# Gates one block further ahead, exponentials between weight copies, two heads' choice moved up, and GpSimd in place of VectorE for the lower activation parts

## The chip, the cores and the metric

One core of a Trainium2 chip runs the kernel. The metric is device time in microseconds (us), median of three runs, lower is better. TensorE (PE) multiplies, VectorE (DVE) and ScalarE (ACT) work elementwise, GpSimd (POOL) works elementwise and issues indirect DMAs, and SyncE's queue (SP) issues the other DMAs. Each engine runs its own instructions in order and waits on semaphores.

## The reference, cut to what matters

A decoder block on 256 tokens of width 1024: two attention mixers, then the PEER channel mixer, which is most of the time. All in float32.

```python
def chunk_fn(xc):                       # 128 tokens at a time
    q = (xc @ wq).reshape(128, 8, 2, 128)
    sc = einsum('thpd,pkd->thpk', q, subkeys)
    sv, si = top_k(sc, 16)              # 16 of 128 keys, both sides
    cand = sv[:, :, 0, :, None] + sv[:, :, 1, None, :]
    cv, ci = top_k(cand.reshape(128, 8, 256), 16)
    e = i1 * 128 + i2                   # the experts chosen
    g = softmax(cv)
    act = gelu(einsum('td,thkd->thk', xc, u[e]))
    return einsum('thk,thkd->td', g * act, v[e])
```

There are 16384 experts. The kernel gathers none: it multiplies all of `u` by the tokens, takes gelu of all of it, multiplies by a gate (the softmax weight where the expert was chosen, else zero), and multiplies all of `v` by the result.

## The kernel before

**Stages.** The two mixers come first, to about 216 us. Then eight query tiles. Then the 128 tiles of `u` (each 128 experts, 512 KB), to about 659 us, then the 128 tiles of `v`, to about 1066 us. `big` holds the activations of all experts, one block of 256 columns (tokens) for each tile.

**Splits.** Each float32 operand is used as two parts in fp32r. For a weight tile ScalarE copies `raw` to `hi` (`loop_hi`, L1197), VectorE subtracts to get `lo` (`loop_lo`, L1682); three slots (`SPLIT = 3`) rotate, so the copy of tile n waits until TensorE has used tile n-3. For an activation block of the `v` stage ScalarE makes `auxh` (`w_hi_gated`, L1224) and VectorE `auxl` (`w_lo`, L1908), in three slots as well. TensorE does three products: high by high, high by low, low by high (`u_tile` L830 to L832, 24 matmuls; `v_tile` L886, 12 matmuls of 512 columns).

**Router.** From the query tiles to `u` tile 62, VectorE chooses keys and pairs (`choose_keys`, `choose_pairs`, `numbers`, `weights`, `addresses`) in an order written out by hand, with the `lo` copies that are due put between by `spread(n)`. GpSimd adds pairs (L2018) and picks (L2028). ScalarE takes three exponentials (`weights_exp`, L1251), after `u` steps 8, 20 and 51 (`EXP_AT`); each has an activation table load before and after it, since gelu needs another table.

**Gates.** For tokens 128 to 255 GpSimd scatters weights into `gate_d` in memory with 128 indirect DMAs (L2038); in the `v` stage SP loads one 64 KB block a tile into a ring of `GRING = 4` (L355), and `gate_block` (L1922) multiplies the activations by it. For tokens 0 to 127 the gates come from one-hot products: for every four tokens `g_group` (TensorE, L843) multiplies `oneB` (ScalarE: `squares_b` L1212, `relu_b` L1218) by `oneA` (VectorE: `keys_equal` L1844, `rows_a` L1852); VectorE sums (`add_parts` L1860) and multiplies (`weigh` L1867). Groups run through the second half of `u` and the first half of `v`: there one group stands before every second `v` tile (the group stage), and the last 67 tiles have none (the plain stage).

**Order in the `v` stage.** In step j VectorE does `w_lo` of block j+2 (which waits for ScalarE's high part), its share of a group, `loop_lo` of tile j+3, and `gate_block` of block j+3. ScalarE does (in even steps `squares_b`), the high part of block j+2, which waits for that block's gate, (in odd steps `relu_b`), and `loop_hi` of tile j+3. SP issues the load of tile j+4 once the `lo` of tile j is made, then the gate load of block j+4 once block j is gated.

Of the kernel before, what the change touches and what calls it, by code (L numbers as in the profile page):

```python
# [23 lines left out]
F32 = mybir.dt.float32  # L24
F32R = mybir.dt.float32r
U32 = mybir.dt.uint32
ALU = mybir.AluOpType
# [3 lines left out]
P = 128  # L31
D = 1024
T = 256
# [3 lines left out]
NH = 8  # L37
# [32 lines left out]
EXP_AT = (8, 20, 51)  # L70
# [20 lines left out]
def build(nc, x_d, wpre_d, u_d, v_d, par_d, cst_d, kep_d, out_d):  # L91
    with ExitStack() as ctx:
# [157 lines left out]
        def S(name):  # L250
            if name not in N:
                N[name] = sem(name)
            return N[name]
# [664 lines left out]
        def _(act):  # L918
# [333 lines left out]
            def weights_exp(z, b, c0, c1):  # L1252

                act.preload_act_table_set(LN_EXP)
                act.wait_ge(S("router_d"), z + 1)
                of_heads = gwt[:, c0 * 16:c1 * 16]
                act.activation(of_heads, of_heads, ACT.Exp, scale=rs2[:, b:b + 1]).then_inc(S("router_exp"), 1)
                act.preload_act_table_set(GELU)

            def u_steps(j0, j1):  # L1260

                for j in range(j0, j1):
                    u_step(0, j)
# [3 lines left out]
            u_steps(EXP_AT[0], EXP_AT[1])  # L1267
            weights_exp(1, 1, NH + 2, 2 * NH)
            u_steps(EXP_AT[1], EXP_AT[2])
            weights_exp(2, 0, 0, NH)  # L1270
            u_steps(EXP_AT[2], ROUTER - 2)
# [47 lines left out]
        def _(dve):  # L1319
# [483 lines left out]
            choose_keys(0)  # L1803
            sc_out(NH - 1)
            spread(2)
# [3 lines left out]
            spread(3)  # L1809
            choose_pairs(NH, 6)  # L1810
            from_best(NH, NH + 2)
            numbers(NH, NH + 2, 6, 9)
            weights(0, NH, NH + 2)
            dve.wait_ge(S("cleared"), 16 * 16)
            addresses(NH, NH + 2)
# [88 lines left out]
            def w_lo(i, b):  # L1904

                s = (V0 + b) % SPLIT
                dve.wait_ge(S("whi_done"), i * UNROLL + (b + 1))
                dve.tensor_tensor(auxl[:, s * T:(s + 1) * T], big[:, bass.ds(i * (UNROLL * T) + b * T, T)],  # L1908
                                  auxh[:, s * T:(s + 1) * T].bitcast(F32), ALU.subtract).then_inc(S("wlo_done"), 1)

            def w_lo_tokens(b, tb, ready, count, done):

                dve.wait_ge(S(ready), count)
                c0 = (V0 + b) % SPLIT * T + tb * P
                dve.tensor_tensor(auxl[:, c0:c0 + P], big[:, b * T + tb * P:b * T + (tb + 1) * P],  # L1915
                                  auxh[:, c0:c0 + P].bitcast(F32), ALU.subtract).then_inc(S(done), 1)

# [6 lines left out]
            w_lo_tokens(0, 0, "whi_tokens", 1, "wlo_tokens")  # L1924
# [4 lines left out]
            w_lo_tokens(0, 1, "whi_done", 1, "wlo_done")  # L1929
            gate_block(0, 2)  # L1930
            w_lo(0, 1)
# [5 lines left out]
            def v_step(i, j):  # L1937
                w_lo(i, j + SPLIT - 1)
                loop_lo(i, V0 + j + SPLIT)
                gate_block(i, j + SPLIT)  # L1940

            def v_step_g(i, j, keys=True, rows=True):
                g = NGRP + 1 + j // 2
                w_lo(i, j + SPLIT - 1)
                if j % 2 == 0:
                    add_parts(i, g, GT)
                    if keys:
                        keys_equal(i, g + 3, GT)
                else:
                    weigh(i, g, GT)  # L1950
                    if rows:
                        rows_a(i, g + 2, GT)
                loop_lo(i, V0 + j + SPLIT)
                gate_block(i, j + SPLIT)
# [4 lines left out]
            each_tile(dve, HALF - 1, lambda i, j: v_step(i, HALF - 2 + j))  # L1959
            w_lo(0, NBLK - 1)  # L1960
# [8 lines left out]
        def _(pool):  # L1969
# [77 lines left out]
            pool.wait_ge(S("keys_chosen"), 2)  # L2047
            pool.wait_ge(S("router"), 1)
            pool.wait_ge(S("chosen"), 1)
            scatter(3)  # L2050
# [24 lines left out]
            scatter(16 * NH - sent[0])  # L2075

# [120 lines left out]
```

## Time and profile before

| | us |
|---|---|
| three runs | 1070.92, 1072.34, 1072.85 |
| median | 1072.34 |
| the profiled execution, as timed | 1071.63 |
| its span in the trace | 1069.6 |

| engine | busy us | share | instructions |
|---|---|---|---|
| TensorE, matmuls | 1047.1 | 98% | 6814 |
| VectorE | 812.1 | 76% | 1631 |
| ScalarE | 629.8 | 59% | 1128 |
| GpSimd | 332.5 | 31% | 227 |

A matmul's busy time runs to the modelled end of its result, so a TensorE that waits a few tenths of a microsecond between tiles still counts as busy. What a tile costs is read from start to start. The times of the trace count from the start of the span.

### The profile page before, as it was taken

To read this page: it belongs to the slowest core of one execution; us is meant where nothing else is said; L and a number is where in the kernel's file an instruction comes from. 1 tells how busy PE (TensorE), PEld (TensorE's weight loads), DVE (VectorE), ACT (ScalarE), POOL (GpSimd) and SP (SyncE) were. 2 spreads that over 40 slices of the span, in tenths; PEclk is the share of its full clock that TensorE was granted. 3 is DMA by queue.
4 is the path that set the end of the run, shared out by engine and by line. 5 is a ranking of instruction groups with operands and counts; after the bars stand their busy time and mean duration, and the time that the engine had idled before them with its cause. 6 is when DMAs were issued, how large, how long until landed. Compare 5 with 4: busy or idle time off the path is not lost.

```text
span 1069.6 us, 21135 instructions
## 1 busy us (share of the span) xinstructions
PE 1047.1 (98%) x6814; PEld 913.8 (85%) x6814; DVE 812.1 (76%) x1631; ACT 629.8 (59%) x1128; POOL 332.5 (31%) x227
## 2 busy tenths in 40 slices
PE   9999999999999999999999999999999999999998
PEld 7798899999999999999999999766676777777775
DVE  7768886788989988977667667887778876666665
ACT  5557776665455445477667666666666654444443
POOL 0011211036268777876877874000000000000000
PEclk9999999999999999999999999999999999999999
DMA  8674646665456666576766766555555576666553
GB/s 339 245 236 134 203 142 212 197 205 170 157 161 174 173 182 188 166 187 168 176 165 169 177 159 173 178 176 169 168 172 177 177 228 200 202 201 201 199 200 106
DMA packets 89473, 198.20 MB, mean 185 GB/s; under 512 B 26320, under 2 KB 42832, under 8 KB 89424
## 3 DMA queue, kind: packets, MB, share of 16 engines
q1 hardware_dynamic: 68544, 188.99, 53.6%
q0 software_dynamic: 20736, 8.46, 6.9%
q8 instruction: 25, 0.41, 0.2%
q10 hardware_dynamic: 144, 0.14, 0.1%
q14 instruction: 24, 0.20, 0.1%
HBM read 187.01 MB, written 10.55 MB: 185 GB/s over the span
## 4 chain that ended last, share of the span: by engine, by line
PE 57%; DVE 15%; issue 14%; ACT 11%; DVEq 1%; ACTq 1%; DMA 0%
PE bank L830 10%; PE bank L832 10%; PE bank L831 10%; ACT hi L1197 7%; DVE lo L1682 6%; DVE big L1922 3%; ACT auxh L1224 3%; PE bank L384 2%; PE bank L385 2%; PE bank L386 2%; PE bank L450 2%; PE bank L770 2%; DVE gsum L1860 2%; DVE oneA L1852 2%; PE bank L454 1%
## 5 line engine op out<-in xcount | busy, mean ns | idle before, releaser
L1682 DVE TENSOR_TENSOR lo<-raw,hi 128x1024 fp32r<-128x1024 f32 x253 | 320.6, 1271 | 100.4 <-ACT hi L1197 99.7
L1197 ACT ACTIVATE hi<-raw 128x1024 fp32r<-128x1024 f32 x253 | 266.2, 1052 | 155.4 <-PE bank L832 152.4
L830 PE MATMUL bank<-xhi,hi 128*128 128x256 f32 x1024 | 292.4, 286 | 3.5 <-DVE lo L1682 2.3
L832 PE MATMUL bank<-xhi,lo 128*128 128x256 f32 x1024 | 290.6, 284 | 0.0
L831 PE MATMUL bank<-xlo,hi 128*128 128x256 f32 x1024 | 290.4, 284 | 0.0
L2038 POOL DMA_INDIRECT gate_d<-chosen_w,chosen_at x128 | 236.2, 1845 | 73.7 <-issue 48.2
L830 PEld LDWEIGHTS bank<-xhi,hi 128*128 128x128 f32 x1024 | 197.4, 193 | 4.0 <-ACT hi L1197 3.5
L831 PEld LDWEIGHTS bank<-xlo,hi 128*128 128x128 f32 x1024 | 197.2, 193 | 0.0
L832 PEld LDWEIGHTS bank<-xhi,lo 128*128 128x128 f32 x1024 | 197.0, 192 | 0.0
L886 PE MATMUL bank<-hi,auxh 128*128 128x512 f32 x504 | 168.3, 415 | 1.8 <-DVE auxl L1915 0.4
L886 PE MATMUL bank<-lo,auxh 128*128 128x512 f32 x504 | 156.9, 392 | 0.0
L1224 ACT ACTIVATE auxh<-big 128x256 fp32r (+1 forms) x127 | 53.0, 418 | 175.5 <-DVE big L1922 175.5
L886 PE MATMUL bank<-hi,auxl 128*128 128x512 f32 x504 | 155.7, 390 | 0.0
L886 PEld LDWEIGHTS bank<-hi,auxh 128*128 128x128 f32 x504 | 85.1, 188 | 46.3 <-DVE auxl L1908 33.1
L1908 DVE TENSOR_TENSOR auxl<-big,auxh 128x256 fp32r<-128x256 f32 x127 | 54.0, 425 | 83.8 <-ACT auxh L1224 83.8
L886 PEld LDWEIGHTS bank<-lo,auxh 128*128 128x128 f32 x504 | 94.6, 188 | 21.6
L886 PEld LDWEIGHTS bank<-hi,auxl 128*128 128x128 f32 x504 | 94.6, 188 | 21.5
L1330 DVE TENSOR_TENSOR lo<-raw,hi 128x1024 fp32r<-128x1024 f32 x73 | 90.1, 1244 | 26.6 <-ACT hi L931 26.3
L931 ACT ACTIVATE hi<-raw 128x1024 fp32r<-128x1024 f32 x73 | 77.1, 1058 | 46.8 <-PE bank L454 19.2
L1212 ACT ACTIVATE oneB<-kep,eT 128x128 fp32r<-128x128 f32 x256 | 81.1, 389 | 0.0
L384 PE MATMUL bank<-xhi,hi 128*128 128x256 f32 x192 | 56.2, 293 | 0.0
L385 PE MATMUL bank<-xlo,hi 128*128 128x256 f32 x192 | 54.2, 283 | 0.0
(393 smaller groups left out, 1493.2 us busy)
## 6 DMA issues: line engine op xcount, KB each, us to landing
raw<-u_d SPq DMA_DIRECT2D x128, 512.0 KB, 3.4
raw<-v_d SPq DMA_DIRECT2D x128, 512.0 KB, 3.4
raw<-wpre_d SPq DMA_DIRECT2D x70, 512.0 KB, 4.4
gate_d<-big POOLq DMA_DIRECT2D x16, 512.0 KB, 5.4
gring<-gate_d SPq DMA_DIRECT2D x128, 64.0 KB, 3.0
big<-wpre_d SPq DMA_DIRECT2D x8, 512.0 KB, 8.3
gate_d<-chosen_w,chosen_at POOLq DMA_INDIRECT x128
big<-x_d SPq DMA_DIRECT2D x4, 256.0 KB, 4.3
```

The costliest lines, as they stand in the source:

```text
L384: pe.matmul(out, wh, xh, start=(k == 0), stop=False)
L830: pe.matmul(out, wh, xhi[:, k, :], start=(k == 0), stop=False)
L831: pe.matmul(out, wh, xlo[:, k, :], start=False, stop=False)
L832: m = pe.matmul(out, wl, xhi[:, k, :], start=False, stop=(k == KT - 1))
L886: m = pe.matmul(bank[2 * b + f][:, :], a_, w_[:, s, f * 512:(f + 1) * 512], start=(first and st_ == 0), stop=False, skip_group_check=True)
L931: act.activation(hi[:, slot(n), :], raw[:, splits(n) % RING, :], ACT.Copy).then_inc(hi_done, 1)
L1197: act.activation(hi[:, slot(n), :], raw[:, splits(n) % RING, :], ACT.Copy).then_inc(hi_done, 1)
L1212: m = act.activation(oneB[:, g % 2, t, :], iota, ACT.Square, bias=i2, scale=-1.0)
L1224: act.activation(auxh[:, s * T:(s + 1) * T], big[:, bass.ds(i * (UNROLL * T) + b * T, T)], ACT.Copy).then_inc(S("whi_done"), 1)
L1330: dve.tensor_tensor(lo[:, slot(n), :], raw[:, splits(n) % RING, :], hi[:, slot(n), :].bitcast(F32), ALU.subtract).then_inc(lo_done, 1)
L1682: dve.tensor_tensor(lo[:, slot(n), :], raw[:, splits(n) % RING, :], hi[:, slot(n), :].bitcast(F32), ALU.subtract).then_inc(lo_done, 1)
L2038: pool.indirect_dma_start(gate_d, bass.IndirectOffsetOnAxis(chosen_at[:, d:d + 1], 0), chosen_w[:, P + d:P + d + 1], None, compute_op=ALU. ...
```

## The change

Four edits, all of order or place; no operation of the computation is added or taken away.

1. `gate_block` in the `v` stage runs four blocks ahead in place of three; the first four blocks are gated before the loop.
2. `w_lo` and `w_lo_tokens` move from VectorE to GpSimd, after its last scatter.
3. `weights_exp` puts the weight copy of step j between gelu and the table load, and the copy of step j+1 between the exponential and the table load back; the places are 4, 18 and 50.
4. VectorE's pair choice, numbers, weights and addresses of the first two heads come before `choose_keys(15)` and `choose_keys(0)`, with six `lo` copies before their end in place of nine. GpSimd issues five scatters in place of three before it waits for the last keys.

```diff
@@ -67,7 +67,7 @@
 HALF = NBLK // 2
 GRING = 4
 EARLY = 7
-EXP_AT = (8, 20, 51)
+EXP_AT = (4, 18, 50)
 
 
 PARAMS = dict(g2=8, qg=64, kgc=64, kgs=128, posk=16, posv=16, w2k=128, w2v=128, subk=256, gw=192)
@@ -1251,11 +1251,15 @@
             act.wait_ge(S("h_saved"), 16 * TB)
             def weights_exp(z, b, c0, c1):
 
+                j = EXP_AT[z]
                 act.preload_act_table_set(LN_EXP)
+                loop_hi(0, N_PRE + j + SPLIT)
                 act.wait_ge(S("router_d"), z + 1)
                 of_heads = gwt[:, c0 * 16:c1 * 16]
                 act.activation(of_heads, of_heads, ACT.Exp, scale=rs2[:, b:b + 1]).then_inc(S("router_exp"), 1)
+                loop_hi(0, N_PRE + j + 1 + SPLIT)
                 act.preload_act_table_set(GELU)
+                gelu_pair(0, j + 1, 0)
 
             def u_steps(j0, j1):
 
@@ -1264,11 +1268,11 @@
 
             u_steps(0, EXP_AT[0])
             weights_exp(0, 1, NH, NH + 2)
-            u_steps(EXP_AT[0], EXP_AT[1])
+            u_steps(EXP_AT[0] + 2, EXP_AT[1])
             weights_exp(1, 1, NH + 2, 2 * NH)
-            u_steps(EXP_AT[1], EXP_AT[2])
+            u_steps(EXP_AT[1] + 2, EXP_AT[2])
             weights_exp(2, 0, 0, NH)
-            u_steps(EXP_AT[2], ROUTER - 2)
+            u_steps(EXP_AT[2] + 2, ROUTER - 2)
             for j in range(ROUTER - 2, ROUTER):
                 loop_hi(0, N_PRE + j + SPLIT)
             act.wait_ge(S("bank67_read"), 2)
@@ -1800,19 +1804,19 @@
 
             keys_ready()
             spread(1)
-            choose_keys(0)
             sc_out(NH - 1)
-            spread(2)
+            choose_pairs(NH, 4)
+            from_best(NH, NH + 2)
+            numbers(NH, NH + 2, 4, 6)
+            weights(0, NH, NH + 2)
+            dve.wait_ge(S("cleared"), 16 * 16)
+            addresses(NH, NH + 2)
             dve.wait_ge(S("sc_out"), NH)
             choose_keys(2 * NH - 1)
             keys_ready()
-            spread(3)
-            choose_pairs(NH, 6)
-            from_best(NH, NH + 2)
-            numbers(NH, NH + 2, 6, 9)
-            weights(0, NH, NH + 2)
-            dve.wait_ge(S("cleared"), 16 * 16)
-            addresses(NH, NH + 2)
+            spread(8)
+            choose_keys(0)
+            spread(9)
             for z in range(3):
                 choose_pairs(NH + 2 + 2 * z, 12 + 3 * z)
             from_best(NH + 2, 2 * NH)
@@ -1901,47 +1905,29 @@
 
             V0 = N_PRE + NBLK
 
-            def w_lo(i, b):
-
-                s = (V0 + b) % SPLIT
-                dve.wait_ge(S("whi_done"), i * UNROLL + (b + 1))
-                dve.tensor_tensor(auxl[:, s * T:(s + 1) * T], big[:, bass.ds(i * (UNROLL * T) + b * T, T)],
-                                  auxh[:, s * T:(s + 1) * T].bitcast(F32), ALU.subtract).then_inc(S("wlo_done"), 1)
-
-            def w_lo_tokens(b, tb, ready, count, done):
-
-                dve.wait_ge(S(ready), count)
-                c0 = (V0 + b) % SPLIT * T + tb * P
-                dve.tensor_tensor(auxl[:, c0:c0 + P], big[:, b * T + tb * P:b * T + (tb + 1) * P],
-                                  auxh[:, c0:c0 + P].bitcast(F32), ALU.subtract).then_inc(S(done), 1)
-
             def gate_block(i, m):
 
                 dve.wait_ge(gate_in[m % GRING], i * (16 * (UNROLL // GRING)) + 16 * (m // GRING + 1))
                 of_block = big[:, bass.ds(i * (UNROLL * T) + (m * T + P), P)]
                 dve.tensor_tensor(of_block, of_block, gring[:, m % GRING, :], ALU.mult).then_inc(S("gated"), 1)
 
-            w_lo_tokens(0, 0, "whi_tokens", 1, "wlo_tokens")
             add_parts(0, NGRP, GT)
             keys_equal(0, NGRP + 3, GT)
             gate_block(0, 0)
             gate_block(0, 1)
-            w_lo_tokens(0, 1, "whi_done", 1, "wlo_done")
             gate_block(0, 2)
-            w_lo(0, 1)
+            gate_block(0, 3)
             dve.wait_ge(S("bank45_read"), NH + NBLK // 2)
             weigh(0, NGRP, GT)
             rows_a(0, NGRP + 2, GT)
             loop_lo(0, N_PRE + NBLK - 1 + SPLIT)
 
             def v_step(i, j):
-                w_lo(i, j + SPLIT - 1)
                 loop_lo(i, V0 + j + SPLIT)
-                gate_block(i, j + SPLIT)
+                gate_block(i, j + GRING)
 
             def v_step_g(i, j, keys=True, rows=True):
                 g = NGRP + 1 + j // 2
-                w_lo(i, j + SPLIT - 1)
                 if j % 2 == 0:
                     add_parts(i, g, GT)
                     if keys:
@@ -1951,13 +1937,13 @@
                     if rows:
                         rows_a(i, g + 2, GT)
                 loop_lo(i, V0 + j + SPLIT)
-                gate_block(i, j + SPLIT)
+                gate_block(i, j + GRING)
 
             each_tile(dve, HALF - 16, v_step_g)
             for j in range(HALF - 16, HALF - 2):
                 v_step_g(0, j, keys=j < HALF - 8, rows=j < HALF - 6)
-            each_tile(dve, HALF - 1, lambda i, j: v_step(i, HALF - 2 + j))
-            w_lo(0, NBLK - 1)
+            each_tile(dve, HALF - 2, lambda i, j: v_step(i, HALF - 2 + j))
+            loop_lo(0, V0 + NBLK - 1)
             dve.wait_ge(S("h_back"), 16 * TB)
             for z, (b, c, w) in enumerate(out_parts_v):
                 dve.wait_ge(S("sum_ready"), z + 1)
@@ -2044,10 +2030,10 @@
                 pair_sum(c)
             pick(NH)
             pick(NH + 1)
-            pool.wait_ge(S("keys_chosen"), 2)
             pool.wait_ge(S("router"), 1)
             pool.wait_ge(S("chosen"), 1)
-            scatter(3)
+            scatter(5)
+            pool.wait_ge(S("keys_chosen"), 2)
             pair_sum(2 * NH - 2)
             pair_sum(2 * NH - 1)
             scatter(8)
@@ -2074,6 +2060,26 @@
                     scatter(1)
             scatter(16 * NH - sent[0])
 
+            V0 = N_PRE + NBLK
+
+            def w_lo(i, b):
+
+                s = (V0 + b) % SPLIT
+                pool.wait_ge(S("whi_done"), i * UNROLL + (b + 1))
+                pool.tensor_tensor(auxl[:, s * T:(s + 1) * T], big[:, bass.ds(i * (UNROLL * T) + b * T, T)],
+                                  auxh[:, s * T:(s + 1) * T].bitcast(F32), ALU.subtract).then_inc(S("wlo_done"), 1)
+
+            def w_lo_tokens(b, tb, ready, count, done):
+
+                pool.wait_ge(S(ready), count)
+                c0 = (V0 + b) % SPLIT * T + tb * P
+                pool.tensor_tensor(auxl[:, c0:c0 + P], big[:, b * T + tb * P:b * T + (tb + 1) * P],
+                                  auxh[:, c0:c0 + P].bitcast(F32), ALU.subtract).then_inc(S(done), 1)
+
+            w_lo_tokens(0, 0, "whi_tokens", 1, "wlo_tokens")
+            w_lo_tokens(0, 1, "whi_done", 1, "wlo_done")
+            each_tile(pool, NBLK - 1, lambda i, j: w_lo(i, j + 1))
+
     return nc
```

## Rows read from the trace of the kernel before

**Rows 1.** Windows: stretch, its length, busy us (count) per engine, clock, DMA, GB/s
```profile
560.00:655.00 95.00, 95.00 (x799) 95.00 (x798) 66.06 (x92) 66.17 (x123) 73.95 (x42) 1.00 0.70 170
665.00:756.00 91.00, 86.24 (x378) 64.88 (x377) 73.07 (x134) 58.15 (x118) 0.00 (x0) 1.00 0.55 175
869.00:960.00 91.00, 90.96 (x371) 67.02 (x370) 58.21 (x95) 42.13 (x62) 0.00 (x0) 1.00 0.63 203
306.70:310.10 3.40, 3.35 (x16) 3.38 (x17) 3.40 (x8) 0.00 (x0) 3.10 (x2) 0.51 0.68 190
```

**Rows 2.** Timeline, group stage: start, us, engine, line, what [idle <-who]
```profile
695.08 0.42 ACT L1224 ACTIVATE auxh<-big 128x256 fp32r x1 [2.02 <-DVE big L1922]
...
695.40 0.61 ACT L1218 ACTIVATE oneB<-oneB 128x512 fp32r<-128x512 f32 x1
...
696.12 0.64 PE L843 MATMUL bank<-oneA,oneB 128*128 128x128 f32 x4 [0.36 <-issue]
```

**Rows 3.** TensorE's timeline: an unstalled group and tile, and the last group
```profile
663.32 0.56 PE L843 MATMUL bank<-oneA,oneB 128*128 128x128 f32 x4
...
666.53 0.62 PE L886 MATMUL bank<-hi,auxh 128*128 128x512 f32 x2
...
866.38 0.63 PE L843 MATMUL bank<-oneA,oneB 128*128 128x128 f32 x4
...
866.86 0.67 PE L886 MATMUL bank<-hi,auxh 128*128 128x512 f32 x2
```

**Rows 4.** Timeline, plain stage: one tile
```profile
941.15 0.62 PE L886 MATMUL bank<-lo,auxh 128*128 128x512 f32 x2
...
942.49 0.42 ACT L1224 ACTIVATE auxh<-big 128x256 fp32r x1 [1.58 <-DVE big L1922]
...
942.98 0.61 PE L886 MATMUL bank<-hi,auxl 128*128 128x512 f32 x2
...
943.05 0.42 DVE L1908 TENSOR_TENSOR auxl<-big,auxh 128x256 fp32r<-128x256 f32 x1 [0.68 <-ACT auxh L1224]
...
943.53 0.30 PEld L886 LDWEIGHTS bank<-hi,auxh 128*128 128x128 f32 x2 [0.36 <-DVE auxl L1908]
```

**Rows 5.** TensorE's timeline: the last two tiles
```profile
1058.50 0.47 PE L901 MATMUL bank<-hi,auxh 128*128 128x512 f32 x1
...
1061.37 0.47 PE L901 MATMUL bank<-hi,auxh 128*128 128x512 f32 x1 [1.93 <-DVE auxl L1908]
```

**Rows 6.** Groups by line, VectorE, 665 to 756 us: the lower parts
```profile
L1908 DVE TENSOR_TENSOR auxl<-big,auxh 128x256 fp32r<-128x256 f32 x27 | 11.5, 425 | 18.3 <-ACT auxh L1224 18.3
```

**Rows 7.** Timeline: GpSimd's 128x256 subtraction, and a VectorE copy beside GpSimd
```profile
234.90 1.47 POOL L1997 TENSOR_TENSOR xlo<-big,xhi 128x256 fp32r<-128x256 f32 x1 [1.16 <-ACT xhi L949]
...
241.38 0.74 POOL L1997 TENSOR_TENSOR xlo<-big,xhi 128x256 fp32r<-128x256 f32 x1 [0.55 <-ACT xhi L949]
...
292.20 1.76 DVE L1682 TENSOR_TENSOR lo<-raw,hi 128x1024 fp32r<-128x1024 f32 x1
```

**Rows 8.** Timeline, router stage: copy, table load, VectorE's waits, TensorE's stalls
```profile
293.45 1.06 ACT L1197 ACTIVATE hi<-raw 128x1024 fp32r<-128x1024 f32 x1 [1.82 <-PE bank L832]
...
295.01 1.28 ACT L1254 ACT_TABLE_LOAD   x1
...
299.04 1.22 DVE L1682 TENSOR_TENSOR lo<-raw,hi 128x1024 fp32r<-128x1024 f32 x1 [2.18 <-ACT hi L1197]
...
306.75 0.55 PE L830 MATMUL bank<-xhi,hi 128*128 128x256 f32 x1 [1.89 <-DVE lo L1682]
...
337.27 1.98 DVE L1682 TENSOR_TENSOR lo<-raw,hi 128x1024 fp32r<-128x1024 f32 x1 [1.10 <-ACT hi L1197]
...
358.69 0.35 PE L830 MATMUL bank<-xhi,hi 128*128 128x256 f32 x1 [1.25 <-ACT hi L1197]
```

**Rows 9.** Timeline: GpSimd's longest instruction of the router stage
```profile
305.49 3.70 POOL L2038 DMA_INDIRECT gate_d<-chosen_w,chosen_at  x1 [0.30 <-issue]
```

**Rows 10.** DMA issues: what, queue, count, KB each, us to landing
```profile
gring<-gate_d SPq DMA_DIRECT2D x128, 64.0 KB, 3.0
```

## The prediction

> **What bounds the kernel now.** I read the windows first, for each engine's busy share and the clock, then the timeline of one repeated pattern in each stage, then the starts of TensorE's instructions, because its busy time hides waits below half a microsecond.
>
> In the windows [rows 1] the columns after the length are TensorE's matmuls, its weight loads, VectorE, ScalarE and GpSimd. In the second half of `u` (560 to 655 us) TensorE is busy all the time at full clock: nothing there can be gained. In the group stage of `v` (665 to 756) it is busy 86.24 of 91 us, VectorE 73.07, ScalarE 58.15, GpSimd 0. No engine is full, so a chain of waits sets the pace.
>
> The chain is in the timeline [rows 2]. ScalarE has waited 2.02 us for VectorE's gate (L1922), makes the high part (695.08), only then `relu_b` (695.40 to 696.01), and TensorE's group, which needs `relu_b`, starts at 696.12. The page can't name what released it ("issue"), but the order in the code and 0.11 us between them do. So the gate, the last thing that VectorE does in a step, is the first that ScalarE needs in the next.
>
> How much TensorE loses: at the start of the stage, where the operands are ready, a group and its tile last from 663.32 to 666.53, 3.21 us [rows 3]. Within a tile four pairs of matmuls take 942.98 - 941.15 = 1.83 us, so the six pairs of a tile take 2.745 us [rows 4]. A group and two tiles would need 3.21 + 2.745 = 5.955 us. They get (866.38 - 663.32) / 30 = 6.77 us [rows 3].
>
> In the plain stage the same chain is closed without groups [rows 4]: high part at 942.49 after a wait of 1.58 for the gate, lower part on VectorE at 943.05, and TensorE's next tile at 943.53 when the lower part is there. From tile 61 (866.86, [rows 3]) to the last two (1058.50, [rows 5]) are 65 tiles, 191.64 us, 2.948 each against 2.745. TensorE's busy time there reads 90.96 of 91 [rows 1]; only the starts show the 7%.
>
> In the router stage TensorE has two larger stalls, 1.89 us at 306.75 and 1.25 at 358.69 [rows 8]. Behind the first, the clock is 0.51, the lower of the two levels, for 3.40 us [rows 1].
>
> **Gates four ahead, and lower parts on GpSimd.** They act together. Gating a block a step earlier takes gate and high part out of the chain: ScalarE finds the block gated a whole tile (2.7 us) ago, more than the 2.02 that it waited. The gate's data must be there too: its load is issued when the `lo` of tile j is made and is now needed after the `lo` of tile j+3, three tiles (8.2 us) later, against 3.0 us to landing [rows 10]. The line of SP's queue is not changed; what stands behind the gate load there is the next tile's load, and the wait in front of it (block j gated) is met a tile earlier. The gate's work on VectorE is the same.
>
> VectorE gives up 11.5 us of lower parts in 91 [rows 6]. Per group pair (6.77 us) it was busy 73.07 / 91 x 6.77 = 5.44; without 0.86 it is 4.58. GpSimd has nothing else in this stage. Its 128x256 subtraction of the same shapes took 0.74 us alone and 1.47 when a copy on VectorE ran [rows 7], and a VectorE copy beside GpSimd took 1.76 against 1.22 alone [rows 7, 8]: the two wait for one another, about 0.54 us on VectorE's side for one operation of GpSimd. Bounds for a pair: two lower parts cost VectorE from 0 (they fall into its waits) to 2 x 0.74 = 1.48. I take two collisions, 1.08, since the rows with a copy running are the nearest: 4.58 + 1.08 = 5.66, below 5.955. The rest of ScalarE fits (58.15 / 91 x 6.77 = 4.33). In the plain stage VectorE has 58.21 / 91 x 2.95 = 1.89 a tile, less 0.43, plus 0.54, so 2.00 below 2.745.
>
> Latency, not only throughput: a slot's new high part follows the weight copy that waits for TensorE to leave tile n-3, so it has two tiles, 5.5 us. In it fall ScalarE's copy, at most one group's squares and the high part; all of ScalarE's pair (4.33) less the other step's `relu_b` 0.61 and high part 0.42 [rows 2] bounds them at 3.3, and GpSimd's 1.47 makes 4.8. Behind GpSimd's wait for the high part stand only further lower parts, and only TensorE waits for them. So TensorE becomes the bound of the whole stage.
>
> The terms, from tile 1 on:
> - group stage: 30 x (6.77 - 5.955) = 24.5 us gained;
> - plain stage: 65 x (2.948 - 2.745) = 13.2 gained;
> - the last tile, for which TensorE waits 1.93 [rows 5] on gate, high part and lower part in a row: all made earlier now, 1.9 gained. Behind that tile's weight copy (1.22 on VectorE [rows 8]) GpSimd's subtraction just fits; the bounds are 0.5 and 1.9;
> - tile 0: its two lower parts, of half the width, stand on the path, since nothing of them can be made sooner. Half width on GpSimd is unseen: between 0 and 0.74 - 0.43 = 0.31 each, or against a VectorE gate 0.3 more. I charge 0.3 in all.
>
> The Trainium skill (SBUF — State Buffer, section "SBUF: two separate sides") says that the port pair between VectorE and GpSimd is an exclusive lock, held for the whole instruction, when the VectorE operation has two SBUF inputs and the GpSimd operation reads SBUF. By that rule, the trace agrees: 1.47 against 0.74 is the rest of the copy plus the operation. Both costs of it are in the sum above.
>
> **Exponentials between copies.** Before, two table loads of 1.28 us [rows 8] and the exponential, a short instruction, stood in a row ahead of a weight copy, and VectorE waited 2.18 us for that copy at 299.04. That delay came back at 306.75 as TensorE's stall, with 3.40 us at clock 0.51 behind it, which cost 3.40 x 0.49 = 1.67. Now each copy has at most one table load with the exponential, or one with a gelu, before it, and ScalarE waits 1.82 ahead of a copy anyway [rows 8]. ScalarE's new wait for VectorE's difference stands behind copy j, and what queues behind it is copy j+1; VectorE's pair choice ends before that copy is due. So the first stall, 1.89 + 1.67 = 3.56, can go. The second, 1.25, comes after the second exponential, for whose delayed copy VectorE waited 1.10 at 337.27 [rows 8]; what VectorE gets back there is what can go, 1.1 of it.
>
> **Two heads sooner.** VectorE's work until `lo` copy nine is the same; only the order changes, and GpSimd starts its scatters a few microseconds sooner. Two more scatters go ahead of a wait for the last keys, and pair sums and picks stand behind them. They start earlier than the three did, so I cost them at nothing; if that cover is gone, pair sums come up to one scatter later, 3.7 at the longest [rows 9]. But six copies, not nine, are made before addresses and the next choice of keys, so the copy of tile 9 comes barely in time. What this costs lies between 0 and a stall as the one now seen, 3.56; I take 0.7, as VectorE keeps within a few tenths of due. Router stage in all: 3.56 + 1.1 - 0.7 = 4.0 gained (0 to 5).
>
> **Sum.** 24.5 + 13.2 + 1.9 - 0.3 + 4.0 = 43.3 us. The profiled execution took 1071.63 (span 1069.6), 0.7 below the median. 1071.6 - 43.3 = 1028.3, and against the median 1029.
>
> **Rivals.**
> A. *VectorE stays the bound, by the port.* If each lower part on GpSimd shuts VectorE out for its whole 0.74, and GpSimd's turns fall so that VectorE can't use its waits, the pair is 4.58 + 1.48 = 6.06 plus one 0.68 wait as in [rows 4] that still ends late, 6.74 at most. The middle, 6.4, gains 11 in place of 24.5: 1042. For it: VectorE operations with two SBUF inputs fill most of its pair. Against: sum and reduction read PSUM, VectorE's waits are left, and the two engines alternate in the rows. The Trainium skill (Perfetto Trace Analysis, "Optimizing Scalar/DVE Operations") warns that since the two share a port, moving work between them might not help; by that rule this rival is the outcome.
> B. *Slower: GpSimd becomes the bound of the `v` stage.* Its operation with a running register offset in a loop is not seen before. It decides from a mean spacing of 6.77 / 2 = 3.4 us a lower part in the group stage and 2.95 in the plain one. At the 3.70 of its longest row [rows 9], it is 30 x (7.40 - 6.77) + 65 x (3.70 - 2.948) = 68 more, less 4 from the router: 1136. Against: 1.47 with a collision is half of that.
> C. *The router gains nothing:* the stall moves to the copy after the new addresses. 1029 + 4 = 1033.
> D. *The edits don't do what they say:* gates land late, so ScalarE waits as before, and the router stall stays. 1072. Against: 8.2 us for a 3.0 us load.
>
> **How the numbers follow.** Forecast 0.58, A 0.22, C 0.12, B 0.05, D 0.03. Faster by over 0.2% (about what a measurement of this kernel can tell from no change) are forecast, A and C: 0.92; D is the same, 0.03; B is slower, 0.05. The low end is the forecast with the router's whole 5.3 and no charge at tile 0, and tenths to spare: 1025. The high end takes C and A past its middle: 1047. Out are B, D and the far part of A, below 0.2.
>
> **What would show it.** Right: group pairs near 5.96 us and plain tiles near 2.745; ScalarE's waits at L1224 on the gate gone, and its wait at the weight copy on TensorE's L886 in their place; lower parts on GpSimd with durations of 0.74 and about 1.3 to 1.9; no wait of TensorE longer than 1 us between 290 and 400 us and no clock of 0.5 there. Wrong: TensorE waiting for `auxl` from GpSimd, VectorE's copies at 1.76 in every pair with pairs at 6.1 or more, GpSimd's spacing near a tile's time, or a stall at the ninth or tenth `u` tile.

## The result and the profile after

| | before | after |
|---|---|---|
| median, us | 1072.59 | 1025.41 |
| runs, us | | 1025.34 to 1025.73 |
| span of the profiled execution | 1069.6 | 1023.6 |

The ratio is 0.9562 [0.9545, 0.9578], 4.4% faster. 47.2 us came off the median, 46.0 off the span; 43.3 were forecast, a median of 1029 in a range of 1025 to 1047. The changed kernel was run again beside the second group of experiments: 1025.59, ratio 0.9572 [0.9556, 0.9588], span 1023.8. One slow execution of `a_no_pool` (5321.45 us, mean clock 0.18, the profiled one) and one of the kernel before beside it (2014.76) are left out of every comparison here.

The first section of the page of the changed kernel, and its chain of work that ended last (shares of the span):

```profile
PE 1015.7 (99%) x6814; PEld 922.0 (90%) x6814; DVE 812.7 (79%) x1502; ACT 629.4 (61%) x1128; POOL 492.3 (48%) x356
...
PE 94%; DVE 4%; ACT 1%; DMA 0%; issue 0%; SPq 0%; POOL 0%; ACTq 0%; POOLq 0%; DVEq 0%
```

The chain now lies on TensorE for 94% of the span. GpSimd has 160 us more work than before. VectorE has 129 instructions fewer, and yet as many busy microseconds: 812.7 against 812.1.

Windows of the changed kernel, with the columns of [rows 1]: the group stage, a stretch of the plain stage, and the place of the first router stall.

```profile
665.00:756.00 91.00, 91.00 (x433) 76.16 (x432) 81.40 (x124) 68.39 (x140) 35.09 (x31) 1.00 0.61 201
840.00:931.00 91.00, 91.00 (x403) 75.33 (x403) 66.22 (x69) 45.42 (x67) 46.03 (x34) 1.00 0.67 216
296.60:300.00 3.40, 3.40 (x28) 3.40 (x29) 3.40 (x18) 0.92 (x2) 2.86 (x2) 1.00 0.71 213
```

TensorE is busy in all of both 91 us, with 433 and 403 matmul records where there were 378 and 371. The 3.40 us at clock 0.51 [rows 1] have no successor: behind the first wait that is left, 0.44 us at 296.60, the clock is 1.00.

TensorE's timeline after, in the order of the stages: the three waits left in the router stage, the start of `v` (group, tile 0, group), the group at the end of the group stage, the last two tiles.

```profile
296.60 0.36 PE L830 MATMUL bank<-xhi,hi 128*128 128x256 f32 x1 [0.44 <-DVE lo L1686]
...
354.98 0.35 PE L830 MATMUL bank<-xhi,hi 128*128 128x256 f32 x1 [0.57 <-DVE lo L1686]
...
358.45 0.36 PE L830 MATMUL bank<-xhi,hi 128*128 128x256 f32 x1 [0.38 <-DVE lo L1686]
...
655.43 0.56 PE L843 MATMUL bank<-oneA,oneB 128*128 128x128 f32 x4
...
656.58 0.70 PE L886 MATMUL bank<-hi,auxh 128*128 128x512 f32 x2 [0.59 <-POOL auxl L2076]
...
659.73 0.56 PE L843 MATMUL bank<-oneA,oneB 128*128 128x128 f32 x4
...
837.53 0.56 PE L843 MATMUL bank<-oneA,oneB 128*128 128x128 f32 x4
837.92 0.68 PE L886 MATMUL bank<-hi,auxh 128*128 128x512 f32 x2
...
1014.81 0.39 PE L901 MATMUL bank<-hi,auxh 128*128 128x512 f32 x1
...
1015.49 0.39 PE L901 MATMUL bank<-hi,auxh 128*128 128x512 f32 x1
```

From the second group of `v` to this last one are 30 pairs in 837.53 - 659.73 = 177.80 us, 5.927 each (6.77 before [rows 3]). From 837.92 to 1014.81 are 65 tiles in 176.89 us, 2.721 each (2.948 before [rows 3, 5]). The last but one and last tile (1014.81, 1015.49) follow without the gap of 1.93 [rows 5].

The waits over the whole kernel (who waited for what: us in total, times, longest):

```profile
POOL auxl L2069 <- ACT auxh L1224: 196.2, 126, 3.5
...
ACT hi L1197 <- PE bank L886: 132.5, 124, 1.8
```

ScalarE's wait for the gate has no line left. Before, it was 175.5 us in 125 waits: 1.58 in a plain tile [rows 4], and in the group stage 2.02 [rows 2] and 0.42 in turn. ScalarE now waits for TensorE to leave a weight buffer, and so does everything behind it. GpSimd waits for its inputs; TensorE's wait for GpSimd at 656.58 is the only one in `v`.

### The profile page after: what moved, and what is told of

It is laid out like the page before. It is cut to its first block, busy times and chain, and to the rows that moved or that the text cites. A ratio compares the mean times of both kernels' runs of the same rounds, so it can differ in the third digit from the quotient of the medians.

```text
span 1023.6 us, 21177 instructions
## 1 busy us (share of the span) xinstructions
PE 1015.7 (99%) x6814; PEld 922.0 (90%) x6814; DVE 812.7 (79%) x1502; ACT 629.4 (61%) x1128; POOL 492.3 (48%) x356
## 4 chain that ended last, share of the span: by engine, by line
PE 94%; DVE 4%; ACT 1%; DMA 0%; issue 0%; SPq 0%; POOL 0%; ACTq 0%; POOLq 0%; DVEq 0%
PE bank L886 34%; PE bank L830 11%; PE bank L832 11%; PE bank L831 11%; PE bank L384 2%; PE bank L843 2%; PE bank L385 2%; PE bank L386 2%; PE bank L450 2%; PE bank L770 2%; DVE lo L1686 2%; PE bank L454 1%; PE bank L466 1%; PE bank L468 1%; PE bank L467 1%; PE bank L747 1%
## 5 line engine op out<-in xcount | busy, mean ns | idle before, releaser
L831 PE MATMUL bank<-xlo,hi 128*128 128x256 f32 x1024 | 289.7, 283 | 0.0
L2024 POOL DMA_INDIRECT gate_d<-chosen_w,chosen_at x128 | 233.7, 1826 | 69.4 <-issue 46.5
L2069 POOL TENSOR_TENSOR auxl<-big,auxh 128x256 fp32r<-128x256 f32 x127 | 161.0, 1267 | 196.2 <-ACT auxh L1224 196.2
L886 PE MATMUL bank<-hi,auxh 128*128 128x512 f32 x504 | 157.3, 393 | 0.6 <-POOL auxl L2076 0.6
L886 PEld LDWEIGHTS bank<-hi,auxh 128*128 128x128 f32 x504 | 92.2, 188 | 18.4 <-issue 0.7
L1912 DVE TENSOR_TENSOR big<-big,gring 128x128 f32 (+1 forms) x128 | 87.8, 688 | 0.0
L1864 DVE TENSOR_REDUCE gsum<-bank 128x256 f32<-128x512 f32 x64 | 44.0, 688 | 16.8 <-PE bank L843 16.6
```

The costliest lines, as they stand in the source:

```text
L831: pe.matmul(out, wh, xlo[:, k, :], start=False, stop=False)
L886: m = pe.matmul(bank[2 * b + f][:, :], a_, w_[:, s, f * 512:(f + 1) * 512], start=(first and st_ == 0), stop=False, skip_group_check=True)
L1912: dve.tensor_tensor(of_block, of_block, gring[:, m % GRING, :], ALU.mult).then_inc(S("gated"), 1)
L2024: pool.indirect_dma_start(gate_d, bass.IndirectOffsetOnAxis(chosen_at[:, d:d + 1], 0), chosen_w[:, P + d:P + d + 1], None, compute_op=ALU. ...
L2069: pool.tensor_tensor(auxl[:, s * T:(s + 1) * T], big[:, bass.ds(i * (UNROLL * T) + b * T, T)], auxh[:, s * T:(s + 1) * T].bitcast(F32), AL ...
```

## The experiments

Each was run beside the kernel before on the same chip (medians of 1070.69 to 1070.83 us there). The edits shown are cut to the lines that matter. The experiments compare stages by starts of TensorE. The `u` stage is the time from the last start of L453 before it (268.1 us, before and after) to the first group of `v`: 659.12 - 268.1 = 391.0 before, 655.43 - 268.1 = 387.3 after. That leaves out the first microseconds of the program, which differ by up to 1.2 us between executions.

**Lower parts back on VectorE** (`a_no_pool`), all else as after:

```
 def v_step(i, j):                       # VectorE's step of the v stage
+    w_lo(i, j + SPLIT - 1)              # was GpSimd's
     loop_lo(i, V0 + j + SPLIT)
```

> The changed kernel with the lower activation parts back on VectorE (gates four ahead and the router edits kept). Theory 1, the chain: the wait of ScalarE for the gate was what set the pace, and gates further ahead end it alone; VectorE needs 5.44 us of a pair of 5.93 and 1.7 of a plain tile of 2.72, so the time stays that of the changed kernel, 1025 to 1027 us, pairs at 5.93. Theory 2, the load: VectorE's share has to fall as well, since its waits don't vanish; pairs at 6.3 or more, 1036 to 1045 us.

Measured: 1026.0 us, ratio 0.9576 [0.9558, 0.9595]. Its trace is of the execution left out, so it was run again for another:

> The changed kernel with the lower activation parts on VectorE, once more, for its trace. Theory 1, the chain: 1025 to 1026.5 us, group pairs at 5.93 us and plain tiles at 2.72 as in the changed kernel; VectorE busy for about 5.44 of 5.93 us of a pair and no 0.83 us gate products. Theory 2, the load: some pairs run late behind VectorE, a mean pair of 6.0 us or more.

Measured: 1025.91, ratio 0.9578 [0.956, 0.9595], span 1023.8, the same as after's on that chip (1025.59, 1023.8). Its window of the group stage, and the groups by line of VectorE there (busy us, mean ns):

```profile
665.00:756.00 91.00, 91.00 (x433) 76.19 (x432) 84.82 (x156) 68.33 (x140) 0.00 (x0) 1.00 0.61 202
```
```profile
L1686 DVE TENSOR_TENSOR lo<-raw,hi 128x1024 fp32r<-128x1024 f32 x31 | 37.9, 1222 | 3.7 <-ACT hi L1197 3.7
L1912 DVE TENSOR_TENSOR auxl<-big,auxh 128x256 fp32r<-128x256 f32 x31 | 13.1, 422 | 2.2 <-ACT auxh L1224 2.2
...
L1926 DVE TENSOR_TENSOR big<-big,gring 128x128 f32 x31 | 8.8, 285 | 0.0
```

Copy and gate of the changed kernel there, and GpSimd's lower part:

```profile
L1686 DVE TENSOR_TENSOR lo<-raw,hi 128x1024 fp32r<-128x1024 f32 x31 | 38.4, 1239 | 0.8
L2069 POOL TENSOR_TENSOR auxl<-big,auxh 128x256 fp32r<-128x256 f32 x31 | 35.1, 1132 | 56.7 <-ACT auxh L1224 56.7
L1912 DVE TENSOR_TENSOR big<-big,gring 128x128 f32 x31 | 17.0, 548 | 0.0
```

(L1912 is the lower part in the experiment and the gate in the changed kernel.) VectorE does all of it at 84.82 of 91 us busy, 93%, and TensorE still has no gap. With GpSimd, VectorE is rid of 13.1 us, but its 31 gates take 17.0 instead of 8.8, so 8.2 come back; it is busy 81.40, only 3.4 less (copies are 0.5 longer; the rest was not taken apart). GpSimd makes all lower parts, as the change says, and next to gates four ahead that is worth nothing that these runs can tell.

**Gates a tile later again** (`b_no_ahead`), GpSimd and router as after:

```
-gate_block(i, j + GRING)      # GRING = 4
+gate_block(i, j + SPLIT)      # SPLIT = 3, as before
```

> The changed kernel with gates three ahead as before (lower parts on GpSimd and the router edits kept). Theory 1, the chain: the plain stage keeps the cycle gate, high part, weight copy, VectorE's copy, gate, about 2.95 us a tile, since the lower part is not in it; in the group stage VectorE no longer waits 0.69 for the high part, pairs at about 6.4; 1052 to 1060 us. Theory 2, the load: lower parts off VectorE bring most of the gain, 1026 to 1040 us.

Measured: 1057.59, ratio 0.9875 [0.9857, 0.9893], span 1054.3. Over the group stage a pair takes (851.14 - 659.51) / 30 = 6.39 us. The plain stage in its timeline:

```profile
931.27 0.30 PEld L886 LDWEIGHTS bank<-hi,auxh 128*128 128x128 f32 x2 [0.38 <-POOL auxl L2067]
...
932.83 0.42 ACT L1224 ACTIVATE auxh<-big 128x256 fp32r x1 [1.58 <-DVE big L1912]
...
933.42 0.74 POOL L2067 TENSOR_TENSOR auxl<-big,auxh 128x256 fp32r<-128x256 f32 x1 [2.21 <-ACT auxh L1224]
...
934.21 0.30 PEld L886 LDWEIGHTS bank<-hi,auxh 128*128 128x128 f32 x2 [0.35 <-POOL auxl L2067]
```

It is the chain of [rows 4] with GpSimd in VectorE's place: the wait of 1.58 for the gate is back, and a tile takes 934.21 - 931.27 = 2.94 us. By spans, undoing the gates' distance loses 1054.3 - 1023.6 = 30.7 of the 46.0 us. Of the 15.3 that are left the router has 3.6 and the group stage 203.06 - 191.63 = 11.4: GpSimd's part is worth that here, where VectorE is still in the chain (6.39 a pair instead of 6.77), and nothing once the gates are earlier, as `a_no_pool` shows. In the plain stage it is worth nothing even here: 65 tiles and the start take 1043.24 - 851.14 = 192.10 us, before 1058.50 - 866.38 = 192.12.

**Router as before** (`c_no_router`) and **router alone** (`d_only_router`), the same edits undone and kept:

```
-EXP_AT = (4, 18, 50)          # c: this undone, and the order of ScalarE's instructions,
+EXP_AT = (8, 20, 51)          # heads and scatters; d: these edits alone, on the kernel before
```

> The changed kernel with exponentials, heads and scatters in the order of before; the v stage as changed. Theory 1: the stages are independent, and it is slower than the changed kernel by what group 32 came earlier in its trace, 3.7 us: 1029 us. Theory 2: the last scatters, now later, delay the first gates of the v stage too: 1031 us or more.

> The kernel before with the router edits alone (exponentials between copies, two heads sooner). Theory 1, stages independent: 3.7 us faster than before, 1069 us. Theory 2, the v stage's chain absorbs or adds to it: no gain, 1072 us, or more than 5 us.

Measured: `c` 1028.74, ratio 0.9601 [0.9577, 0.9626]; `d` 1068.51, ratio 0.9976 [0.9964, 0.9987]. In `d`, the `u` stage takes 655.42 - 268.1 = 387.3, the same as after; 3.7 us are gained. Its span, 1067.2, is only 2.4 below that of before: the last two tiles and what follows take 1067.2 - 1054.6 = 12.6 us instead of 11.1, since the clock was low behind the wait of 1.93 for the last tile, which it was not in the trace of before (windows in the last section). In `c` the stalls of [rows 8] are back (the second is 1.24 us at 358.56):

```profile
306.61 0.36 PE L830 MATMUL bank<-xhi,hi 128*128 128x256 f32 x1 [1.88 <-DVE lo L1682]
```

Its `u` stage takes 391.3. So router and `v` stage add up; neither hides the other.

**The router's two edits apart.** `e_exp_in_row` puts table load, exponential and table load back in a row; `f_old_heads` keeps them between the copies, and undoes "two heads sooner":

```
 # e, ScalarE                             # f, VectorE and GpSimd
-loop_hi(0, N_PRE + j + SPLIT)            -choose_pairs(NH, 4)
-loop_hi(0, N_PRE + j + 1 + SPLIT)        +choose_pairs(NH, 6)
-gelu_pair(0, j + 1, 0)                   -scatter(5)
                                          +scatter(3)
```

> The changed kernel with table load, exponential and table load back in a row behind steps 4, 18 and 50; the two heads stay sooner. Theory 1, the exponentials' place is what counts: weight copies 8, 22 and 54 of the u stage come 1.1 us late, TensorE's stall at the ninth tile grows from 0.44 to about 1.5 us and the one near 355 us from 0.57 to about 1.5: 1027 to 1029 us. Theory 2, the heads' order counts: 1025.4 us.

> The changed kernel with the order of heads and scatters of before; exponentials between copies, at steps 8, 20 and 50. Theory 1, the exponentials count: VectorE's wait of 2.18 us at 299 falls below 0.7, TensorE's stall of 1.89 us to 0.3 or less, no clock of 0.5: 1025 to 1026 us. Theory 2, the heads count: the stall stays near 1.9 us and the time at 1028 to 1029.

Measured: `e` 1027.36, ratio 0.9586 [0.9569, 0.9603]; `f` 1025.15, ratio 0.9567 [0.9551, 0.9583]. ScalarE's timeline in the changed kernel, then in `e`:

```profile
283.43 1.28 ACT L1255 ACT_TABLE_LOAD   x1
284.74 1.06 ACT L1197 ACTIVATE hi<-raw 128x1024 fp32r<-128x1024 f32 x1
285.71 0.30 ACT L1259 ACTIVATE big<-big 128x32 f32<-128x32 f32 x1
287.62 1.06 ACT L1197 ACTIVATE hi<-raw 128x1024 fp32r<-128x1024 f32 x1 [1.61 <-PE bank L832]
288.70 1.28 ACT L1261 ACT_TABLE_LOAD   x1
```
```profile
286.80 1.28 ACT L1254 ACT_TABLE_LOAD   x1
288.10 0.32 ACT L1257 ACTIVATE big<-big 128x32 f32<-128x32 f32 x1
288.44 1.28 ACT L1258 ACT_TABLE_LOAD   x1
289.73 1.06 ACT L1197 ACTIVATE hi<-raw 128x1024 fp32r<-128x1024 f32 x1
```

In a row, table load, exponential and table load take 289.73 - 286.80 = 2.9 us in front of the next copy. TensorE's larger waits in `e`, and below them those in `f`:

```profile
298.21 0.36 PE L830 MATMUL bank<-xhi,hi 128*128 128x256 f32 x1 [1.07 <-DVE lo L1682]
...
356.90 0.35 PE L830 MATMUL bank<-xhi,hi 128*128 128x256 f32 x1 [0.88 <-DVE lo L1682]
```
```profile
305.06 0.36 PE L830 MATMUL bank<-xhi,hi 128*128 128x256 f32 x1 [0.28 <-DVE lo L1686]
...
354.75 0.36 PE L830 MATMUL bank<-xhi,hi 128*128 128x256 f32 x1 [0.51 <-DVE lo L1686]
```

A third follows in each, as in the changed kernel (0.38 in `e`, 0.37 in `f`). The sums are 2.33 and 1.16, after 1.39. Of `e`'s 1.9 longer span 1.0 is in the `u` stage; the rest was lost in the first 269 us, where the program does the same. `f` has its exponentials at 8, 20 and 50. With `c` and after, the `u` stages make a square:

| `u` stage, us | exponentials in a row | between copies |
|---|---|---|
| heads as before | `c`: 659.28 - 268.0 = 391.3 | `f`: 654.93 - 268.1 = 386.8 |
| two heads sooner | `e`: 657.39 - 269.05 = 388.3 | after: 387.3 |

Each edit alone gains, 3.0 us the heads (their exponentials also stand at other tiles, 5 and 19 instead of 8 and 20) and 4.5 the place of the exponentials, and they don't add up: on top of the second, the first gives nothing, and costs about 0.5. That rests on one trace of `f`; in five more traces with the router of after the `u` stage takes 387.4 to 387.7 (`g_pad1` has 388.8). Both take away the same stall: from 1.88 in `c` it falls to 1.07 in `e`, where no low clock follows, and to 0.28 in `f`.

**How much room the port has** (`g_pad1`, `h_pad2`): nothing is left out; GpSimd does one or two extra 128x256 sums after each lower part, whose results nobody uses.

```
+for z in range(1):            # h_pad2: range(2)
+    pool.tensor_tensor(pad[:, z, :], kep[:, 0:T], kep[:, 0:T], ALU.add)
```

> The changed kernel with one more 128x256 addition on GpSimd behind each lower part of blocks 1 to 127 (it reads constants and writes a spare buffer; nothing of the result depends on it). Theory P, time on the port adds up: VectorE's operations with two SBUF inputs hold about 4.1 us a pair, four of GpSimd 0.56 each, 6.35 in place of 5.93: group stage 12.6 us longer; plain tile 1.4 + 1.12 = 2.5, below 2.72: about 1038 us. Theory Q, each engine's own time only: GpSimd needs 4 x 0.70 = 2.8 of 5.93 us: 1025.5.

> The same with two more additions a block. Theory P: pairs at 4.1 + 6 x 0.56 = 7.46, plain tiles at 1.4 + 3 x 0.56 = 3.08: 46 + 23 = 69 us longer, about 1094 us, slower than the kernel before. Theory Q: GpSimd needs 3 x 0.70 = 2.1 us a tile, below 2.72: 1025.5.

Measured: `g` 1040.21, ratio 0.9709 [0.9692, 0.9725]; `h` 1065.18, ratio 0.9942 [0.9925, 0.9959]. Windows of `g`, then of `h`, and a stretch of `h` that is all plain stage:

```profile
665.00:756.00 91.00, 88.73 (x405) 70.74 (x404) 91.00 (x114) 63.31 (x130) 67.10 (x58) 1.00 0.57 185
```
```profile
665.00:756.00 91.00, 83.34 (x376) 65.64 (x375) 91.00 (x105) 58.42 (x121) 84.65 (x81) 1.00 0.52 170
...
890.00:1010.00 120.00, 117.30 (x502) 92.72 (x501) 92.57 (x84) 57.17 (x85) 120.00 (x126) 1.00 0.64 207
```

In the group stage VectorE is busy 91.00 of 91 in both, and a pair takes 6.38 us in `g` ((852.52 - 661.00) / 30) and 6.83 in `h` ((864.47 - 659.71) / 30), against 5.93. VectorE's own program is unchanged, so its time has grown only by longer instructions. One such stretch in `g`, VectorE and then GpSimd beside it:

```profile
705.54 1.76 DVE L1687 TENSOR_TENSOR lo<-raw,hi 128x1024 fp32r<-128x1024 f32 x1
707.22 0.69 DVE L1913 TENSOR_TENSOR big<-big,gring 128x128 f32 x1
```
```profile
705.40 0.81 POOL L2070 TENSOR_TENSOR auxl<-big,auxh 128x256 fp32r<-128x256 f32 x1 [0.88 <-ACT auxh L1225]
706.18 1.59 POOL L2074 TENSOR_TENSOR pad<-kep 128x256 f32<-128x256 f32 x1
```

The lower part began 0.14 us ahead of the copy, which takes 1.76 instead of 1.22; the sum came in during the copy, and the gate behind it takes 0.69 instead of 0.28. Over the window copies take 1736 ns on average and gates 706. That is rival A, made on purpose.

In the plain stage (in `h` all of 890 to 1010 us) `g` loses nothing: 65 tiles from the last group (852.52) to the last two (1029.81) are 177.29 us, as in the changed kernel (837.53 to 1014.81, 177.28). `h` needs 188.0 there, and GpSimd is busy in all of the 120 us: there it is the bound, rival B, at three operations a tile.

The theory that port times simply add gave 1038 and 1094. It comes within 2 us for one extra operation and overstates two by 29: its group stage was to grow by 46 us and its plain stage by 23, and they grew by 204.8 - 177.8 = 27 and 188.0 - 177.3 = 11. Six operations of GpSimd a pair were to cost VectorE 6 x 0.56 = 3.4 us; its instructions are longer by 2.3 (a copy 0.53, a gate 0.42, twice each; `weigh`, L1872, 0.84 instead of 0.41). The reduction from PSUM is not lengthened (677 ns in both, 691 in the changed kernel).

Of `g`'s 15.0 us of longer span, 13.7 are in the group stage; 1.3 were lost before `v`, where nothing is padded (a stall of 0.72 us at 414), and stay unexplained.

**Weight copies before choices** (`i_copies_first`), and **only what the runs had shown to matter** (`j_gates_exps_only`: the kernel before, gates four ahead, exponentials between copies, and the copies first):

```
+spread(7)                                # i: copies due, ahead of choose_keys(2 * NH - 1)
+spread(10)                               # j: ahead of the other heads' choose_pairs
+spread(27)                               # i, j: ahead of the last key choices
-spread(26 + (11 * c) // 7)
+spread(max(28, 26 + (11 * c) // 7))
```

> The changed kernel with three of VectorE's weight copies put ahead of a choice of keys (that of the ninth tile ahead of choose_keys(15), those of steps 27 and 28 ahead of and behind choose_keys(1)). Theory 1: these copies were TensorE's last stalls in the router stage, 0.44 + 0.57 + 0.38 us: about 1024.1. Theory 2: VectorE is full there, and the stall moves to the next copy: 1025.4.

> The kernel before with the gates four ahead and the exponentials between copies alone (lower parts on VectorE, heads and scatters as before), and the copies of steps 9, 27 and 28 ahead of choices. Theory 1: the other two edits add nothing, so it is as fast as the changed kernel without its stalls: 1023.8 to 1024.5. Theory 2: they count: 1026 or more.

Measured: `i` 1024.86, ratio 0.9566 [0.9553, 0.958]; `j` 1024.39, ratio 0.9569 [0.9554, 0.9584]. The larger of two stalls in `i`, then the only one in `j`:

```profile
305.69 0.36 PE L830 MATMUL bank<-xhi,hi 128*128 128x256 f32 x1 [0.42 <-DVE lo L1686]
```
```profile
366.28 0.36 PE L830 MATMUL bank<-xhi,hi 128*128 128x256 f32 x1 [0.38 <-DVE lo L1686]
```

`i` lies between its two theories: it takes away the three waits (1.39) and gets two others, 0.42 and 0.37 at 367.00, so the stall moved and became smaller. Its `u` stage is 655.07 - 268.5 = 386.6, 0.7 less than after. `j`, with its exponentials at 8, 20 and 50, has one wait, and 654.49 - 268.2 = 386.3. It has neither GpSimd's lower parts nor the heads moved, and is no slower than the changed kernel: 1.0 us less by the medians, of runs on two chips whose ratios to before (0.9562 and 0.9569) don't tell them apart.

## Why the prediction was right, and where it was not

**What bounds the kernel** was read rightly. `b_no_ahead` brings back the wait of 1.58 and the tile of 2.94, with nothing undone but the gate's distance.

**The terms**, by spans:

| term | forecast | measured | from |
|---|---|---|---|
| router stage | 4.0 | 3.7 | 659.12 - 655.43 |
| tile 0 | -0.3 | -0.1 | (663.32 - 659.12) - (659.73 - 655.43) |
| group stage | 24.5 | 25.3 | 203.06 - 177.80 |
| first plain start | | 0.1 | 0.48 - 0.39 |
| plain stage | 13.2 | 14.75 | 191.64 - 176.89 |
| last tiles | 1.9 | 2.3 | (1069.6 - 1058.50) - (1023.6 - 1014.81) |
| sum | 43.3 | 46.0 | |

- *Plain stage, mis-sized by 1.5 us.* The step "four pairs of matmuls take 942.98 - 941.15 = 1.83 us, so the six pairs of a tile take 2.745" took the floor from a tile that had just been held up: its pairs there start 0.46, 0.46, 0.45 and 0.46 apart. An undisturbed tile takes 2.721, six pairs of 0.4535: 0.024 less, 65 times.
- *Group stage.* The same error, in one of its two tiles, is 0.024 of the 0.028 by which a pair came out below 5.955; the 0.028, 30 times, are 0.8 us. The 3.21 for group and tile [rows 3], taken where nothing had waited, was right: 5.927 - 2.721 = 3.206.
- *Last tiles.* The wait of 1.93 went, as forecast, and the first matmuls of the two tiles take 0.39 instead of 0.47 [rows 5]. The last 0.2 were not traced. What this wait costs differs between executions: in `d_only_router` the clock was low behind it and 1.5 us more were lost.
- *Tile 0.* TensorE waits 0.59 for GpSimd's L2076 at 656.58, where it waited 0.43 for VectorE before; the group and tile take 4.30 instead of 4.20. With the lower parts on VectorE it is 4.19 (`a_no_pool_again`: 659.92 - 655.73). The charge was 0.3, of bounds from 0 up.
- *Router.* First stall 1.89 with a low clock, forecast to go for a charge of 0.7: it went and left 0.44 at 296.60. Second, forecast to lose 1.1 of 1.25: it and the 0.37 behind it (362.16 in the trace of before) became 0.57 + 0.38, so 0.7 was gained. The two errors nearly cancel. Of the 3.1 us that the first stall gives back, about 1.7 is the low clock behind it.

**The range** was 1025 to 1047, and 1025.41 is 3.6 us below the forecast and 0.4 above the low end. That it lies inside is in part luck. The terms named for the low end, the router's whole 5.3 in place of 4.0 and no charge of 0.3 at tile 0, make 1029 - 1.6 = 1027.4, and "tenths to spare" don't reach 1025. And what came was not those terms, since the router gave 3.7 and tile 0 cost 0.1: 2.3 us came from the floor of the two stages, 0.4 from the last tiles and 0.2 from tile 0, less 0.3 of the router. Against the profiled execution of before the forecast was 1028.3, and 1025.42 was measured.

**The step that was wrong** is "They act together", of gates four ahead and lower parts on GpSimd. `a_no_pool_again` has the gates four ahead without the other, and the whole gain. The prediction's own numbers could have said so. Per pair VectorE was busy 5.44 us before, which is already below the 5.955 that TensorE needs. Only the order was the trouble, not the amount. The arithmetic went on to subtract 0.86 and add 1.08 for two collisions, 5.66, and did not ask what 5.44 would do. Measured are 84.82 / 91 x 5.927 = 5.52 with all on VectorE and 5.30 with GpSimd.

**The collisions**: the number taken, 0.54 us for each operation of GpSimd, is a copy's (1.76 against 1.22). In the group stage the copies hardly collide (mean 1239 ns against 1222), and half of the gates do. Timeline of the changed kernel, group stage:

```profile
690.90 1.22 DVE L1686 TENSOR_TENSOR lo<-raw,hi 128x1024 fp32r<-128x1024 f32 x1
...
691.12 1.59 POOL L2069 TENSOR_TENSOR auxl<-big,auxh 128x256 fp32r<-128x256 f32 x1 [0.84 <-ACT auxh L1224]
...
692.03 0.83 DVE L1912 TENSOR_TENSOR big<-big,gring 128x128 f32 x1
...
695.00 0.28 DVE L1912 TENSOR_TENSOR big<-big,gring 128x128 f32 x1
```

GpSimd asks at 691.12 and its subtraction is over only at 692.71, 0.59 after VectorE's copy ends; the gate behind that copy then takes 0.83 instead of 0.28, 0.55 more. So it is one collision of 0.54 a pair and not two, the price right and the count wrong. The Trainium skill (SBUF — State Buffer, "SBUF: two separate sides") calls the port an exclusive lock held for a whole instruction, and these rows agree: 1.59 is the rest of the copy (1.00) and 0.59 of its own, and the gate waits for that.

**Rival A** did not come true, and its chance of 0.22 was not wild: one more operation of GpSimd for each tile is enough (`g_pad1`, 6.38 us a pair, close to the 6.4 that A was priced at). The Trainium skill (Perfetto Trace Analysis, "Optimizing Scalar/DVE Operations") warns that moving work between the two might not help because they share a port. Beside gates four ahead it did not help (1025.59 against 1025.91), though not as A had it: nothing was lost either. With the gates at their old distance it did help, by 11.4 us (`b_no_ahead`).

**"Two heads sooner"** was costed at -0.7 by way of tile 9. The square of the router's runs has it costing 0.5 us of the `u` stage, beside exponentials between copies. The sign was right, but the prediction saw no use in it, and alone it has one: 3.0 us.

**A wait read as every tile's.** The 2.02 us that ScalarE waited for the gate [rows 2] is that of every second tile of the group stage; the others waited 0.42. The forecast used 2.02 only as a bound, so no term changes.

**A wrong description.** The text of the change ahead of the prediction has copy j between the gelu and the table load. In the code and in ScalarE's timeline above the order is table load, copy j, exponential, copy j+1, table load back, gelu. No number of the prediction used it, as at most one table load stands ahead of a copy in either order.

## What to carry to other kernels

When no engine is full, follow one pattern of the timeline for the instruction that comes last in one engine's step and is first needed in the next one's: issuing it one step earlier, with no work taken from any engine, brought the whole gain of the `v` stage, 42 of 46 us. Before moving work to another engine, ask whether the busy time of the first one, without the move, already fits under the floor; here 5.44 under 5.96 did, and the move bought nothing. Take a floor from a tile with no wait ahead of it, and measure stages from start to start: the busy share here read 90.96 of 91 us while 0.23 of 2.95 us a tile were lost.

## What the hardware showed beyond that

- A collision at the shared port costs a short instruction as much as a long one: gates in the plain stage (840 to 1010 us) take 829 ns on average in place of 285, GpSimd's subtractions 1381 ns in place of 740. VectorE's 128x1024 copies hardly pay in the group stage of the changed kernel, but 0.51 us each on average in `g_pad1`.
- Work on GpSimd that no other engine waits for can slow the whole kernel: one sum of about 0.7 us in each tile, whose result nobody reads, cost 14.6 us (1040.21 - 1025.59), 13.7 of them in the group stage, where GpSimd itself was busy 67.10 of 91 us.
- Behind a stall of 1.89 us TensorE's granted clock was 0.51 for 3.40 us [rows 1], and behind 1.88 in `c_no_router` 0.52 for as long, from about 0.7 us after the stall. Behind the wait of 1.93 for the last tile it was 0.53 for 3.40 us in `d_only_router` and 1.00 in the kernel before. The windows in that order:

```profile
307.30:310.70 3.40, 3.40 (x19) 3.40 (x18) 3.40 (x12) 0.00 (x0) 3.10 (x3) 0.52 0.77 259
```
```profile
1057.70:1061.10 3.40, 3.40 (x10) 2.62 (x9) 0.69 (x1) 0.00 (x0) 0.00 (x0) 0.53 0.22 82
```
```profile
1061.30:1065.00 3.70, 3.63 (x16) 3.05 (x17) 1.38 (x2) 0.00 (x0) 0.00 (x0) 1.00 0.19 71
```

So stalls of about the same length were followed by the lower level in some cases and not in others; what decides was not found. The clock was 1.00 behind the 1.24 of `c_no_router` (358.50 to 362.00), and behind the 1.07 of `e_exp_in_row`:

```profile
298.20:301.60 3.40, 3.39 (x28) 3.40 (x29) 3.40 (x18) 0.29 (x2) 2.87 (x2) 1.00 0.68 194
```

A stall that shrinks from 1.89 to 0.44 thus gave back more than its length: 1.89 + 3.40 x 0.49 - 0.44 = 3.1 us.

- These stretches also make most of the spread of the kernel before. Of 28 executions of it beside the experiments, one had a mean clock of 1.000 (1069.21 us), 18 had 0.998 (1069.91 to 1071.72) and nine 0.997 (1072.39 to 1073.68). One stretch of 3.4 us at half the clock is 0.0016 of 1070 us, two are 0.0032, so by estimate these are none, one and two of them; only one execution, with one, was traced. The five executions of `after_again` all have 1.000 and lie within 0.9 us.
